# Causal masking in a stick-breaking attention layer: from mask matmuls on TensorE to selects on GpSimd

## What is computed

```python
z = jnp.einsum('bhqd,bhkd->bhqk', qb, k) * scale
strict = key_pos[None, :] < q_pos[:, None]
log_beta = jax.nn.log_sigmoid(z)
log_fail = jnp.where(strict, jax.nn.log_sigmoid(-z), 0.0)
between = lax.cumsum(log_fail, axis=3, reverse=True) - log_fail
w = jnp.where(strict, jnp.exp(log_beta + between), 0.0)
return jnp.einsum('bhqk,bhkd->bhqd', w, v)
```

## Time and profile before

| | us |
|---|---|
| median of 3 runs | 1988.41 (1987.72 to 1989.64) |
| profiled execution | 1991.74 |
| its span, first to last instruction | 1990.0 |
| stick-breaking stages | 200 to 318 and 1680 to 1798 in the span |

### The profile page before, as it was taken

One profiled execution on the slowest core, in us unless ns is written; L12 is line 12 of the kernel. 1 busy time (PEld: TensorE's weight loads), 2 busy tenths in 40 slices (PEclk: granted clock), 3 DMA queues, 4 the chain that ended last, 5 costly groups with the idle time before them and its releaser, 6 DMA issues.

```text
span 1990.0 us, 29473 instructions
## 1 busy us (share of the span) xinstructions
PE 1947.4 (98%) x10724; PEld 1675.5 (84%) x10724; DVE 1373.7 (69%) x1900; ACT 1129.3 (57%) x1682; POOL 58.3 (3%) x123
## 2 busy tenths in 40 slices
PE   8999999999999999999999998999999999999998
PEld 6888988888888878888888887888888888978887
DVE  6766666766766785676676678476667667766666
ACT  6555565555555565655555555555556555556553
POOL 2000000000100000000000000000000000000000
PEclk9999999999999999999999999999999999999999
DMA  6555534556555553455555544245555555535553
GB/s 217 194 191 184 167 128 149 194 191 205 170 190 190 160 180 112 148 194 191 200 169 190 190 159 135 85 135 195 191 184 178 190 191 173 180 116 169 190 190 116
DMA packets 243040, 342.31 MB, mean 172 GB/s; under 512 B 12045, under 2 KB 194970, under 8 KB 242970
## 3 DMA queue, kind: packets, MB, share of 16 engines
q1 hardware_dynamic: 242016, 340.29, 52.0%
q10 hardware_dynamic: 954, 1.07, 0.2%
HBM read 340.27 MB, written 1.05 MB: 172 GB/s over the span
## 4 chain that ended last, share of the span: by engine, by line
PE 92%; DVE 4%; ACT 2%; DMA 1%; issue 1%; SPq 0%; POOL 0%; POOLq 0%; ACTq 0%; DVEq 0%
PE psum L473 33%; PE psum L632 32%; PE psum L640 17%; PE psum L929 4%; DVE wlo L437 2%; ACT whi L423 1%; PE psum L504 1%; PE psum L894 1%; PE psum L1569 1%; DVE xT L499 1%; PE psum L971 1%; PE psum L990 1%; PE psum L904 0%; PE psum L1543 0%; PE psum L1239 0%
## 5 line engine op out<-in xcount | busy, mean ns | idle before, releaser
L423 ACT ACTIVATE whi<-raw,gains 128x512 fp32r<-128x512 f32 (+2 forms) x896 | 568.6, 707 | 284.0 <-PE psum L640 210.1
L632 PE MATMUL psum<-xT,whi 128*128 128x512 f32 x2816 | 681.5, 393 | 12.3 <-DVE xT L499 9.8
L437 DVE SCALAR_TENSOR_TENSOR wlo<-raw,gains,whi 128x512 fp32r<-128x512 f32 (+2 forms) x896 | 608.3, 741 | 71.9 <-ACT whi L423 71.7
L632 PEld LDWEIGHTS psum<-xT,whi 128*128 128x128 f32 x2816 | 522.7, 189 | 123.5 <-DVE xT L499 14.0
L640 PEld LDWEIGHTS psum<-xT,wlo 128*128 128x128 f32 x2816 | 349.6, 192 | 7.1
L640 PE MATMUL psum<-xT,wlo 128*128 128x256 f32 x2816 | 351.8, 283 | 0.0
L748 DVE TENSOR_TENSOR gate_in_T<-psum,low 128x512 f32<-128x512 f32 x88 | 60.9, 692 | 353.7 <-ACT low L695 353.0
L473 PE MATMUL psum<-whi,xT 128*128 128x512 f32 (+2 forms) x848 | 270.8, 388 | 9.5 <-DVE mix L1748 2.4
L433 DVE TENSOR_TENSOR wlo<-raw,whi 128x2048 fp32r<-128x2048 f32 x100 | 228.6, 2286 | 43.2 <-ACT whi L419 43.2
L473 PE MATMUL psum<-whi,hidT_hi 128*128 128x512 f32 x640 | 249.0, 389 | 0.0
L473 PE MATMUL psum<-wlo,hidT_hi 128*128 128x512 f32 x640 | 249.0, 389 | 0.0
(11 more groups left out here) (192 smaller groups left out, 1433.4 us busy)
## 6 DMA issues: line engine op xcount, KB each, us to landing
raw<-in_ffn_wi SPq DMA_DIRECT2D x350, 512.0 KB, 4.6
raw<-in_ffn_wo SPq DMA_DIRECT2D x176, 512.0 KB, 4.3
raw<-in_sb_w_in SPq DMA_DIRECT2D x48, 512.0 KB, 4.6
raw<-in_ml_w_in SPq DMA_DIRECT2D x24, 512.0 KB, 4.5
raw<-in_sb_w_out SPq DMA_DIRECT2D x16, 512.0 KB, 4.2
raw<-in_ml_w_out SPq DMA_DIRECT2D x8, 512.0 KB, 4.0
raw<-in_mla_w_out SPq DMA_DIRECT2D x8, 512.0 KB, 4.0
raw<-in_mla_w_in SPq DMA_DIRECT2D x4, 512.0 KB, 4.1
```

Source lines behind the costliest of these rows:

```text
L423: last = act.activation(whi[:, slot, r], raw[:, slot, r], ACT.Copy, scale=gain_col(p.gain + k))
L437: last = dve.scalar_tensor_tensor(wlo[:, slot, r], raw[:, slot, r], gain_col(p.gain + k), hi[:, r], op0=ALU.mult, op1=ALU.subtract)
L632: i = pe.matmul(psum[:, 4 + blk, :], whi[:, slot, k * 2 * FC + blk * P:k * 2 * FC + (blk + 1) * P], xT[:, 4 * part + k, :, :].rearrange("p ...
```

## The change

`mask_pe` is no longer called in the stick-breaking mixer, and the scores are started afresh in their banks. A new list of work for GpSimd, `sb_pool`, runs per layer eight calls of `strict`: on softplus of g = 0 and 1, on the weights of 0 and 1, on softplus of 2 and 3, on the weights of 2 and 3. Each call is three `affine_select` instructions in place on `sb_e[g]`, over 512, 256 and 256 elements per partition, which set the entries that are not strict to zero. softplus_high on ScalarE waits for the select of softplus (`sp_masked`) where it waited for softplus itself; values on PE waits also for the selects of the weights (`w_masked`). softplus_rest on VectorE still follows softplus_high.

```diff
@@ scores(g)
                 if g >= 2:
                     pe.wait_ge(w_done, 4 * s.inst + g - 1)
-                mask_pe(pe, 0, SB_Z[g])
-                scores_pe(pe, g, SB_Z[g], kT, qT, False).then_inc(z_done, 1)
+                scores_pe(pe, g, SB_Z[g], kT, qT, True).then_inc(z_done, 1)
@@ values(g)
-                pe.wait_ge(w_done, 4 * s.inst + (3 if g < 2 else 4))
+                if g < 2:
+                    pe.wait_ge(w_done, 4 * s.inst + 3)
+                pe.wait_ge(w_masked, 4 * s.inst + (2 if g < 2 else 4))
                 pe.wait_ge(proj_read, 2 * (s.block0 + (5 if g < 2 else 6)))
@@ softplus_high(g)
-                act.wait_ge(sp_done, 4 * s.inst + g + 1)
+                act.wait_ge(sp_masked, 4 * s.inst + g + 1)
@@
+        def sb_pool(pool, link):
+            s = [s for s in subs if s.kind == "sb"][pool_sbs[0]]
+            pool_sbs[0] += 1
+
+            def strict(g, done):
+                e = sb_e[:, g, :]
+                for view in (e[:, 0:2 * NCOL].rearrange("p (b a n) -> p b a n", b=2, a=4)[:, :, 2:4, :],
+                             e[:, 0:2 * NCOL].rearrange("p (b a n) -> p b a n", b=2, a=4)[:, :, 0:1, :],
+                             e[:, 2 * NCOL:3 * NCOL].rearrange("p (b a n) -> p b a n", b=2, a=2)[:, :, 0:1, :]):
+                    i = pool.affine_select(out=view, in_=view, compare_op=ALU.is_gt, fill=0.0, base=0,
+                                           pattern=[[0, 2], [0, view.shape[2]], [1, P]], channel_multiplier=-1)
+                i.then_inc(done, 1)
+
+            for kind, g in ((0, 0), (0, 1), (1, 0), (1, 1), (0, 2), (0, 3), (1, 2), (1, 3)):
+                if kind == 0:
+                    pool.wait_ge(sp_done, 4 * s.inst + g + 1)
+                    strict(g, sp_masked)
+                else:
+                    pool.wait_ge(w_done, 4 * s.inst + g + 1)
+                    strict(g, w_masked)
```

More of the change, by code:

```diff
@@ L275, in trunk @@
         shared_banks = [0]
+        pool_sbs = [0]
         abs_done = sem("abs_done")
@@ L280, in trunk @@
         sp_hi_done = sem("sp_hi_done")
+        sp_masked = sem("sp_masked")
+        w_masked = sem("w_masked")
         sp_lo_done = sem("sp_lo_done")
@@ L1851, in lt_pool @@
                                ALU.pow).then_inc(lrms_done, 1)
-        MIXERS = {"sb": {"pe": sb_pe, "act": sb_act, "dve": sb_dve},
+        MIXERS = {"sb": {"pe": sb_pe, "act": sb_act, "dve": sb_dve, "pool": sb_pool},
                   "ml": {"set_up": ml_set_up, "pe": ml_pe, "act": ml_act, "dve": ml_dve, "pool": ml_pool},
```

## The result

The changed kernel takes 1994.91 us (median of six runs, 1994.11 to 1997.90), the kernel before in the same comparison 1988.13 (1987.72 to 1989.64). The ratio is 1.0035, with a 95% interval of 1.0025 to 1.0046: 6.8 us slower, a third of a per cent. The profiled execution took 1995.38 with a span of 1993.5; that of before had 1991.74 and 1990.0. In all six timed runs of the changed kernel the granted clock of TensorE, averaged over the run, was 0.994 to 0.996; in 69 of 72 runs of the kernel before, timed beside the experiments, it was 0.997 to 0.999.

What follows compares the result with a forecast made beforehand. TensorE's queue (PE) was taken to bound the kernel. Per layer -1.32 + 1.55 + 1.80 + 0.38 - 1.32 = +1.09, +2.2 for both, added to the median 1988.41: 1990.6 us, range 1984.5 to 1996.0.

Steps and rivals of the forecast that it cites:

- rival (b): At conv(8) and conv(9), VectorE and GpSimd take turns, ending in the stall before plain(8): +7.4, 1995.8 us; chance 0.22.
- What bounds the kernel, and where the change bites: PE bounds the kernel; at plain(8) it has no slack behind VectorE's evacuation; idle time there forecast as 3.7 us a layer.
- Masks removed, -1.32 and -1.32: PE, scores: two mask calls before plain(8) and two behind it go, 0.66 us each, -1.32 and -1.32 a layer.
- The call, 1.45 us and 0.10 of hand-over: GpSimd's three selects for g = 0, between softplus(0) and softplus_high(0), add 1.45 plus 0.10 for the semaphore: +1.55 us.
- GpSimd held up by conv(8), +1.80: Each of the first call's three selects waits for a VectorE subtraction of conv(8), 0.60 each: +1.80 us.
- VectorE held up, +0.38 in conv(9): VectorE's conv(9) waits for GpSimd's call for g = 1, taken as one small select: +0.38 us.
- The sum at plain(8): Start of plain(8): -1.32 + 1.55 + 1.80 + 0.38; with the masks behind it, -1.32, +1.09 us for a layer.
- Part 3, the covers: Calls other than g = 0 on softplus are covered; softplus_rest(3) has 2.95 us of room before remainder(3), not used up.

Runs made afterwards that it cites:

- e2: Changed kernel without GpSimd's first call in a layer (softplus of group 0), so its output differs; median 1984.18 us, both stick-breaking stages 114.78.
- e6: Changed kernel with VectorE's evac_T(3, 0) moved before softplus(1) and evac_T(3, 1) behind it, both ahead of conv(9); median 1986.97 us.
- e1: Changed kernel with mask matmuls kept for groups 0 and 1, GpSimd selects only for groups 2 and 3; median 1989.41 us, both stages 115.76.
- e3: Kernel before, mask matmuls kept, with GpSimd running the same 16 calls on a spare tile nobody waits for; median 1990.38 us.
- e4: Kernel before, GpSimd idle, with three VectorE additions of 512 columns between conv(9) and evac_T(3, 0); PE waited 1.88 us; median 1993.47 us.
- e5: Kernel before, GpSimd idle, with six VectorE additions between conv(9) and evac_T(3, 0); PE waited 3.69 us; median 2001.03 us.
- before_again: The kernel before, unchanged, profiled once more; profiled run 1987.48 us, latent attention 115.85.
- e8: Changed kernel with a wait on VectorE, so that conv(8) starts only after GpSimd's first call; median 1992.07 us.

## Why the prediction was right and where it failed

The measured 1994.9 us lies in the range (1984.5 to 1996.0), near its upper end. The forecast was 1990.6 and "no change that can be measured"; what came was slower by a measurable 0.35%, which had been given 0.22. That the range holds the result is in part luck: it reaches so far up only for rival (b), whose mechanism did not happen, and the clock, which made up the difference, stands in no term of the sum.

**What bounds the kernel, and where the change bites: right.** The wait stands where the prediction said, before plain(8), once a layer, released by VectorE's evacuation. PE's wait of 3.21 us is within 0.5 of the 3.7 forecast. e2 (114.78 us without the call) and e6 (114.72 with the evacuation taken out of the chain) show that it is this chain, from two sides.

**Masks removed, -1.32 and -1.32: right.** absolute(1) starts at 240.08 where it started at 241.58; the stage began 0.16 earlier, so 1.34 are the masks. e1 gained 1.31 for two.

**The call, 1.45 us and 0.10 of hand-over: right.** 1.39 alone. float32 selects cost no more than the bf16 ones from which they were worked out. The hand-over is 0.07 + 0.02.

**GpSimd held up by conv(8), +1.80: right in kind, too high.** 2.73 - 1.39 = 1.34.

**VectorE held up, +0.38 in conv(9): right.** 0.33 (3.07 against 2.74). The row that seemed to speak against it did not settle it: selects over 256 and 512 elements hold VectorE up where multiplies over 128 hadn't. Why those didn't is not shown. e3 shows it without any dependency. The rule of the Trainium skill (page "SBUF — State Buffer", "Who interferes with whom"), mutual exclusion for the whole instruction, is borne out in both directions, but not in full. The four subtractions (2.73 alone) and the three selects (1.39 alone) need 4.12 us if they never overlap; from 243.42 to 246.85 is 3.43. So by the records, which are rough for GpSimd, 0.69 us of them did overlap.

**The sum at plain(8): right.** -1.34 + 2.80 (call with hold-up and hand-over) + 0.33 = +1.79, where 257.04 against 255.39, with 0.16 for the earlier start of the stage, gives +1.81; predicted were +2.41. PE's wait was forecast as 3.7 and is 3.21. With the masks behind it the layer would be 0.5 us slower than before, better than the forecast's 1.09.

**What was left out: the clock.** Measured are +2.10 and +3.27 us for the two layers. The difference to +0.5, which is 1.6 and 2.8 us, is plain(8) at the lower clock: 7.32 and, in the chain of the second layer, 8.50 us for 24 matmuls that took 5.71. The prediction priced a wait of 3.7 us at its own length. It had the granted clock at 1.00 in the earlier trace rows, and never asked what PE's standing still would do to it. This is the term that the sum had at nothing without a reason. e4 and e5 show a price of 1.5 to 1.6 us where GpSimd does nothing at all; why the second layer of the changed kernel pays 2.8 each time stays open. Rival (b) came close in its total, 1995.8, by another mechanism: its larger interference (+7.4) did not happen.

**The rest.** 2.10 + 3.27 = 5.4 of the 6.8 us. Against before_again the changed kernel's profile is 7.9 us longer: 5.4 in these stages, 1.7 in the latent attention, 1.1 in the first feed-forward stage (which the first profile of the kernel before has too); it started 0.5 earlier. In both of its profiles the latent attention took 117.5, in two of three of before 115.9. Whether the change moves the clock's fall there, or it is chance, stays open: nine more kernels with the same instructions in that stage gave 115.9 (four times), 117.5 (twice), 119.2, 120.6 and 120.9.

**Part 3, the covers: right, but the room shrank.** softplus_rest(3) ended 2.95 us before remainder(3). In the changed kernel it runs from 289.03 to 290.79 and remainder(3) starts at 291.22: 0.4 us are left, since GpSimd's call for group 3 meets conv(13), one subtraction of 2.29 us. The prediction's "one delayed call doesn't use up" was nearly wrong.

## What to carry to other kernels

When work moves off the bounding engine, follow what its reader waits for through every engine back to the bounding one; if that chain has no gap, the saved time comes back as a wait, and the cure is to take the next thing that engine needs out of the chain (here two evacuations placed one step earlier, worth 4.5 and 5.6 us in the two layers against the changed kernel). Price a wait of TensorE by its length and by the clock it may lose (here 1.5 to 2.8 us for a wait of 3.2 us or more). GpSimd selects on SBUF and VectorE instructions with two SBUF inputs should not be put side by side where either is in the chain; here even a deliberate wait of VectorE was faster.

## What the runs showed of the hardware

- TensorE's clock: an idle stretch of PE was followed each time by some microseconds of work at 0.50 (3.4 and 6.0 in the changed kernel) when it had lasted 3.2 us (four times, in two profiles of the changed kernel) and 3.69 us (twice, e5), at a price of 1.5 to 2.8 us; after 1.88 us this happened in two of four cases (e4, e8), after 0.72 us in none of two. In the latent attention PE's longest wait is 2.3 us, and one kernel took 115.9 or 119.2 us there.
- GpSimd: a select of 512 and two of 256 float32 elements per partition take 1.39 us together, up to 2.73 beside four subtractions of VectorE, whose time goes from 2.73 to 3.43.
